# One 512-column product issued as two of 256: the input projections of a hybrid decoder layer on one Trainium2 core

## The chip, the cores and the metric

The kernel runs on one core of one Trainium2 chip. The metric is the device time of one execution in microseconds (us). The kernel before was run three times: 1012.82 us is the median, 1004.70 and 1013.37 us are the ends.

## What is computed

One decoder layer on 512 tokens of width 1024, in float32. It has three sublayers, each closed by a layer norm: a hybrid mixer, cross-attention into 256 memory tokens, and a SwiGLU channel mixer. Only the first one matters here. Cut to its input side:

```python
def hybrid_mixer(x, w_in, b_in, pool_w, ...):
    z = x @ w_in + b_in                       # 1024 -> 8 * 1024 columns
    z_pool, z_lru, z_b, z_c, z_h, z_gate = split(z)
    y_pool = multiscale_pool(z_pool, pool_w, pool_scale)   # grouped 256x256 products
    y_lru = rg_lru(z_lru, ..., w_r, b_r, w_i, b_i, ...) @ lru_w_out   # 128x128 gate heads
    y_conv = gated_short_conv(z_b, z_c, z_h, sconv_w, sconv_w_out)
    gates = sigmoid(z_gate).reshape(s, 3, 1024)
    merged = gates[:, 0] * y_pool + gates[:, 1] * y_lru + gates[:, 2] * y_conv
    return merged @ w_mix_out
```

## The kernel before

Every float32 product is made of three matmuls by the helper `mm3` (lines 843 to 847). Each operand is held as a high part and a low part (`wh`, `wl` for weights, `xT_h`, `xT_l` for the transposed tokens), and one product adds high x high (line 845), high x low (line 846) and low x high (line 847) into the same place of `ps`, the accumulators (8 banks of 512 float32 on 128 partitions). The first argument of each matmul is the stationary operand, a 128x128 block of weights, and the second is the moving operand, a number of token columns. In the trace each matmul has a weight load of its own in front of it, so one `mm3` is three weight loads and three matmuls.

The mixer's input side runs as four passes `a_pass(i)`, i = 0 to 3, each over two blocks of 128 columns of each of the branches (stage A, from 11.6 to 246.5 us of the profiled span). A pass consists of fifteen weight steps in a fixed order: lru0, lru1, pool0, pool1, P1, P5, P6, P2, P7, pool_w, ri, b0, P4, b1, P3. They come in two kinds:

- The steps whose names begin with lru, pool and b are done by `half_unit`: one call goes through 2 column blocks (`l`) and 4 blocks of the inner dimension (`k`), so it makes 8 `mm3`, each with all 512 tokens as moving columns. The steps pool_w (`p_h`, `p_l` moving) and ri (`vr_h`, `vr_l` moving) make 4 `mm3` each, also over 512 tokens, and stand in `a_pass` itself. In pass 0 the lru steps are done by another function, `half_tokens`, already 256 tokens at a time.
- The steps P1 to P7 are done by `product`: 8 `mm3` over 256 columns each (`x_part`, a quarter of `xT`, or sums of such quarters in `ta` and `tb`).

After stage A follow stage B (the gates, steps P1 to P7 again, all of 256 columns, to 374.6 us), the output projections (512 columns), the attention (both sizes), and the channel mixer, whose first part (665 to about 880 us, moving `x`, `xa`, `xb`, `xc`) is of 256 columns and whose second is of 512.

The order on each engine is written out by hand; each engine runs its own list and meets the others at semaphores. A weight step passes through a chain: a DMA brings it in (`raw`, `wx`), ScalarE writes the rounded high part (`wh`, lines 1354, 1410, 1466), VectorE subtracts to get the low part (`wl`, lines 1905, 1981, 2182). The weights have four slots. TensorE waits at the beginning of a step for its low part (`weights_ready`) and gives the slot free on the last matmul of the step (`weights_used`); ScalarE and VectorE also read the accumulators on that signal. So the last matmul of a step is the only one that anybody waits for.

Of the kernel before, what the change touches and what calls it, by code (L numbers as in the profile page):

```python
# [29 lines left out]
P = 128  # L30
# [29 lines left out]
def hybrid_layer(nc, x, mem, w_in, b_in, pool_w, pool_scale, lru_conv_w, lru_conv_b, lru_w_r, lru_b_r,  # L60
# [39 lines left out]
    with ExitStack() as ctx:  # L100
# [24 lines left out]
        xT_h = sb("xT_h", [P, KT, SEQ], F32R)  # L125
        xT_l = sb("xT_l", [P, KT, SEQ], F32R)
# [12 lines left out]
        with ExitStack() as scope:  # L139
            p_h = sb("p_h", [P, 2, SEQ], F32R, scope)  # L140
            p_l = sb("p_l", [P, 2, SEQ], F32R, scope)
            vr_h = sb("vr_h", [P, 2, SEQ], F32R, scope)
            vr_l = sb("vr_l", [P, 2, SEQ], F32R, scope)
# [82 lines left out]
        ps = ctx.enter_context(nc.psum_tensor("ps", [P, 8, 512], F32))  # L226
# [222 lines left out]
        def ri_bank(i, l, g):  # L449
            return A_POOL + g if l == 0 else m_bank(i) + 1 - g  # L450
# [391 lines left out]
        def _(pe):  # L842
            def mm3(dst, st, st_lo_part, mv_, mv_lo_part, start, stop, shared=False):

                nc.tensor.matmul(dst, st, mv_, start=start, stop=False, skip_group_check=shared)  # L845
                nc.tensor.matmul(dst, st, mv_lo_part, start=False, stop=False, skip_group_check=shared)  # L846
                return nc.tensor.matmul(dst, st_lo_part, mv_, start=False, stop=stop, skip_group_check=shared)  # L847
# [69 lines left out]
            def turn_par():  # L917
# [4 lines left out]
                nc.tensor.transpose(ps[:, 7, P:P + 32], rows[0:32, 1, :],  # L922
                                    ident[0:32, 0:32]).then_inc(par_full.sem, 1)

            def half_unit(i, name, bank):

                half = int(name[-1])
                weights_ready("A", 0, a_step(i, name))
                h_, l_ = (a_slot(w, i, name) for w in (wh, wl))
                for l in range(2):  # L930
                    for k in range(4):
                        last = mm3(ps[:, bank + l, :], h_[:, k, l * P:(l + 1) * P], l_[:, k, l * P:(l + 1) * P],
                                   xT_h[:, 4 * half + k, :], xT_l[:, 4 * half + k, :],
                                   half == 0 and k == 0, half == 1 and k == 3)
                last.then_inc(weights_used.sem, 1)

            def a_pass(i):
                j1 = i * 2 + 1
                low, mid = l_bank(i), m_bank(i)
# [38 lines left out]
                h_, l_ = (a_slot(w, i, "pool_w") for w in (wh, wl))  # L978
                for l in range(2):
                    for k in range(2):  # L980
                        last = mm3(ps[:, low + l, :], h_[:, k, l * P:(l + 1) * P], l_[:, k, l * P:(l + 1) * P],
                                   p_h[:, k, :], p_l[:, k, :], k == 0, k == 1)
                last.then_inc(weights_used.sem, 1)

                weights_ready("A", 0, a_step(i, "ri"))
# [2 lines left out]
                h_, l_ = (a_slot(w, i, "ri") for w in (wh, wl))  # L988
                for l in range(2):
                    for g in range(2):  # L990
                        if (l, g) == (1, 1):
                            pe.wait_ge(ac_sum.sem, ac_sum.done(3 * i))
                        last = mm3(ps[:, ri_bank(i, l, g), :], h_[:, g, l * P:(l + 1) * P], l_[:, g, l * P:(l + 1) * P],
                                   vr_h[:, l, :], vr_l[:, l, :], True, True)
                last.then_inc(weights_used.sem, 1)
                pe.wait_ge(ypool.sem, ypool.done(j1))
                half_unit(i, "b0", low)
# [145 lines left out]
            for k in range(4):  # L1143
                k_ready("C", 0, k, k)
                for t in range(TT):
# [6 lines left out]
                    last = accumulate("C", k, 2 * t, t, k == 0, False)  # L1152
# [21 lines left out]
            for h in range(HEADS):  # L1174
# [13 lines left out]
                for half in range(2):  # L1188
# [4 lines left out]
                    h_, l_ = (w_slot(w, "D", s).rearrange("p (k n) -> p k n", k=4) for w in (wh, wl))  # L1193
# [45 lines left out]
            for k, t in ((0, 2), (1, 2), (0, 3), (1, 3), (2, 2), (2, 3), (3, 2), (3, 3)):  # L1239
                if (k, t) == (0, 3):  # L1240
                    pe.wait_ge(ot_full.sem, ot_full.done(2 * HEADS - 1))
                last = accumulate("E", k, e_bank(t), t, k == 0, False)
# [1481 lines left out]
```

## Time and profile before

| | us |
|---|---|
| three runs: median (lowest, highest) | 1012.82 (1004.70, 1013.37) |
| span of the profiled execution | 1006.1 |
| TensorE (PE) busy | 991.6 (99% of the span) |
| weight loads (PEld) busy | 903.4 (90%) |
| VectorE (DVE) busy | 719.5 (72%) |
| ScalarE (ACT) busy | 503.5 (50%) |
| PE in the chain of work that ended last | 87% |

Busy time counts an engine as busy as long as at least one instruction is in it. Matmuls overlap: one of 512 columns is shown with 389 ns, yet the next one starts about 227 ns after it. So neither the busy share nor the duration of one matmul is its price in a row of matmuls; that is read from the starts of the first and the last of a row, and from their count. The granted clock of TensorE is shown in tenths or as a share of full speed. The profiled execution is one execution; its span lies between the lowest and the median run.

### The profile page before, as it was taken

Reading aid. Unit: us, or ns where it says so; the run is one execution under the profiler, and the core shown is the slowest. Engines: PE = TensorE matmul, PEld = TensorE weight load, DVE = VectorE, ACT = ScalarE, POOL = GpSimd, SP = SyncE. Lnnn points to the kernel's source line nnn. Section 1 sums busy time; section 2 is a strip of 40 time slices with the busy share of each in tenths; the row PEclk is TensorE's granted clock in tenths of the full one; section 3 lists DMA queues with packets and bytes.
Section 4 is the critical chain, followed back from the end, with each engine's and each line's share of the span. In section 5 each row is a group of like instructions: output and inputs, shape, how many; then the busy total and the mean of one; then the engine's idle time right before and its main releaser. Section 6 shows DMA issues by size and latency. Waiting matters only on the chain.

```text
span 1006.1 us, 15698 instructions
## 1 busy us (share of the span) xinstructions
PE 991.6 (99%) x6460; PEld 903.4 (90%) x6460; DVE 719.5 (72%) x909; ACT 503.5 (50%) x710; POOL 9.9 (1%) x22
## 2 busy tenths in 40 slices
PE   8999999999999999999999999999999999999997
PEld 8988889898999998888899998889999999988885
DVE  6979798796998885455675554589988888743336
ACT  6673846657575573123454443366554554623232
POOL 1000000000000000000000000000000000000000
PEclk9999999999999999999999999999999999999999
DMA  8243434315333344235163331223434332433212
GB/s 294 66 134 117 148 105 126 126 43 191 118 108 110 99 153 147 66 123 209 43 210 126 126 102 67 84 69 109 139 103 125 100 113 84 141 114 123 83 42 84
DMA packets 92165, 117.46 MB, mean 117 GB/s; under 512 B 3244, under 2 KB 82240, under 8 KB 92096
## 3 DMA queue, kind: packets, MB, share of 16 engines
q1 hardware_dynamic: 89328, 106.97, 32.6%
q0 software_dynamic: 2624, 9.47, 2.8%
q8 instruction: 50, 0.82, 0.3%
q14 instruction: 19, 0.16, 0.0%
q10 hardware_dynamic: 144, 0.05, 0.0%
HBM read 111.23 MB, written 5.24 MB: 116 GB/s over the span
## 4 chain that ended last, share of the span: by engine, by line
PE 87%; DVE 6%; ACT 4%; issue 2%; DMA 0%; DVEq 0%; POOL 0%; ACTq 0%; POOLq 0%
PE ps L845 28%; PE ps L846 28%; PE ps L847 28%; PE ps L874 1%; DVE wl L1981 1%; ACT wh L1410 1%; DVE o L2169 1%; ACT wh L1466 0%; DVE v L2031 0%; DVE wl L2182 0%; DMA raw<-in_w_in 0%; PE ps L1162 0%; PE ps L886 0%; ACT gates L1614 0%; ACT L1450 0%
## 5 line engine op out<-in xcount | busy, mean ns | idle before, releaser
L845 PE MATMUL ps<-xT_h,wh 128*128 128x256 f32 (+1 forms) x512 | 170.6, 333 | 0.4 <-DVE wl L1981 0.4
L846 PE MATMUL ps<-xT_l,wh 128*128 128x256 f32 (+1 forms) x512 | 169.8, 332 | 0.0
L847 PE MATMUL ps<-xT_h,wl 128*128 128x256 f32 (+1 forms) x512 | 169.7, 332 | 0.0
L1905 DVE TENSOR_TENSOR wl<-raw,wh 128x1024 fp32r<-128x1024 f32 x66 | 80.3, 1223 | 112.7 <-ACT wh L1354 112.7
L1354 ACT ACTIVATE wh<-raw 128x1024 fp32r<-128x1024 f32 x66 | 69.4, 1062 | 148.4 <-PE ps L847 136.2
L2182 DVE TENSOR_TENSOR wl<-raw,wh 128x1024 fp32r<-128x1024 f32 x72 | 87.5, 1223 | 54.3 <-ACT wh L1466 54.1
L1466 ACT ACTIVATE wh<-raw 128x1024 fp32r<-128x1024 f32 x72 | 75.5, 1058 | 96.7 <-PE ps L847 65.7
L845 PE MATMUL ps<-wh,st_h 128*128 128x512 f32 x304 | 118.8, 391 | 0.0
L847 PE MATMUL ps<-wh,st_l 128*128 128x512 f32 x304 | 118.3, 389 | 0.0
L846 PE MATMUL ps<-wl,st_h 128*128 128x512 f32 x304 | 118.3, 389 | 0.0
L845 PEld LDWEIGHTS ps<-xT_h,wh 128*128 128x128 f32 x512 | 96.2, 188 | 10.3 <-issue 0.8
L847 PEld LDWEIGHTS ps<-xT_h,wl 128*128 128x128 f32 x512 | 96.7, 189 | 9.5
L846 PEld LDWEIGHTS ps<-xT_l,wh 128*128 128x128 f32 x512 | 96.6, 189 | 9.3
L845 PE MATMUL ps<-xa,wh 128*128 128x256 f32 x368 | 101.9, 277 | 0.4 <-DVE xa L1921 0.4
L846 PE MATMUL ps<-xa,wh 128*128 128x256 f32 x368 | 101.6, 276 | 0.0
L847 PE MATMUL ps<-xa,wl 128*128 128x256 f32 x368 | 101.6, 276 | 0.0
L845 PEld LDWEIGHTS ps<-xa,wh 128*128 128x128 f32 x368 | 69.1, 188 | 1.0 <-DVE xa L1921 0.8
L847 PEld LDWEIGHTS ps<-xa,wl 128*128 128x128 f32 x368 | 69.1, 188 | 0.0
L846 PEld LDWEIGHTS ps<-xa,wh 128*128 128x128 f32 x368 | 69.1, 188 | 0.0
L847 PEld LDWEIGHTS ps<-wh,st_l 128*128 128x128 f32 x304 | 57.1, 188 | 11.8
L845 PEld LDWEIGHTS ps<-wh,st_h 128*128 128x128 f32 x304 | 57.1, 188 | 11.6
L846 PEld LDWEIGHTS ps<-wl,st_h 128*128 128x128 f32 x304 | 57.1, 188 | 11.6
(298 smaller groups left out, 2372.5 us busy)
## 6 DMA issues: line engine op xcount, KB each, us to landing
raw<-in_w_in SPq DMA_DIRECT2D x42, 512.0 KB, 3.8
raw<-in_ffn_w_down SPq DMA_DIRECT2D x11, 1024.0 KB, 4.9
raw<-in_ffn_w_gate SPq DMA_DIRECT2D x20, 512.0 KB, 4.1
wx<-in_w_in SPq DMA_DIRECT2D x16, 512.0 KB, 4.6
gb<-in_ffn_w_up SPq DMA_DIRECT2D x10, 512.0 KB, 3.9
raw<-in_ffn_w_up SPq DMA_DIRECT2D x10, 512.0 KB, 4.3
raw<-in_lru_w_out SPq DMA_DIRECT2D x8, 512.0 KB, 3.5
raw<-in_sconv_w_out SPq DMA_DIRECT2D x8, 512.0 KB, 3.4
```

Source lines behind the costliest of these rows:

```text
L845: nc.tensor.matmul(dst, st, mv_, start=start, stop=False, skip_group_check=shared)
L846: nc.tensor.matmul(dst, st, mv_lo_part, start=False, stop=False, skip_group_check=shared)
L847: return nc.tensor.matmul(dst, st_lo_part, mv_, start=False, stop=stop, skip_group_check=shared)
L874: last = nc.tensor.transpose(ps[:, bank + half, n * P:(n + 1) * P], src[:, tile, k * P:(k + 1) * P], ident[:])
L1354: nc.scalar.activation(w_slot(wh, phase, s, size), src, ACT.Copy).then_inc(w_hi.sem, 1)
L1410: nc.scalar.activation(a_slot(wh, i, name), a_src(i, name), ACT.Copy).then_inc(w_hi.sem, 1)
L1466: nc.scalar.activation(w_slot(wh, phase, n).rearrange("p (k n) -> p k n", k=4), src, ACT.Copy).then_inc(w_hi.sem, 1)
L1905: nc.vector.tensor_tensor(w_slot(wl, phase, s, size), src, w_slot(wh, phase, s, size).bitcast(F32), ALU.subtract).then_inc(w_lo.sem, 1)
L1981: nc.vector.tensor_tensor(a_slot(wl, i, name), a_src(i, name), a_slot(wh, i, name).bitcast(F32), ALU.subtract).then_inc(w_lo.sem, 1)
L2169: nc.vector.scalar_tensor_tensor(out=o[:, l, :], in0=ch[:, l, k:k + SEQ], scalar=par[:, SC_W0 + k, j:j + 1], in1=o[:, l, :], op0=ALU.mult, ...
L2182: nc.vector.tensor_tensor(w_slot(wl, phase, n).rearrange("p (k n) -> p k n", k=4), src, w_slot(wh, phase, n).rearrange("p (k n) -> p k n", ...
```

## The change

A new helper `by_tokens` takes the place of `mm3` in three places: in `half_unit`, in the step pool_w and in the step ri. It calls `mm3` twice, first for the columns of tokens 0 to 255, then for tokens 256 to 511, with the same block of weights. So three matmuls of 512 columns become six of 256, and three weight loads become six. `start` (which clears the place before the first addition) is given to the first half alone, as `product` does already; `stop` goes to both. Waits and signals stay where they were: the signal still stands on the last matmul of the step. No instruction of another engine is changed, and no DMA.

```diff
+            def by_tokens(bank, st, st_lo_part, mv_, mv_lo_part, start, stop):
+
+                for tok in range(2):
+                    part = slice(tok * 256, (tok + 1) * 256)
+                    last = mm3(ps[:, bank, part], st, st_lo_part, mv_[:, part], mv_lo_part[:, part],
+                               start and tok == 0, stop, shared=True)
+                return last
+
             def half_unit(i, name, bank):
...
                     for k in range(4):
-                        last = mm3(ps[:, bank + l, :], h_[:, k, l * P:(l + 1) * P], l_[:, k, l * P:(l + 1) * P],
-                                   xT_h[:, 4 * half + k, :], xT_l[:, 4 * half + k, :],
-                                   half == 0 and k == 0, half == 1 and k == 3)
+                        last = by_tokens(bank + l, h_[:, k, l * P:(l + 1) * P], l_[:, k, l * P:(l + 1) * P],
+                                         xT_h[:, 4 * half + k, :], xT_l[:, 4 * half + k, :],
+                                         half == 0 and k == 0, half == 1 and k == 3)
...
                     for k in range(2):
-                        last = mm3(ps[:, low + l, :], h_[:, k, l * P:(l + 1) * P], l_[:, k, l * P:(l + 1) * P],
-                                   p_h[:, k, :], p_l[:, k, :], k == 0, k == 1)
+                        last = by_tokens(low + l, h_[:, k, l * P:(l + 1) * P], l_[:, k, l * P:(l + 1) * P],
+                                         p_h[:, k, :], p_l[:, k, :], k == 0, k == 1)
...
-                        last = mm3(ps[:, ri_bank(i, l, g), :], h_[:, g, l * P:(l + 1) * P], l_[:, g, l * P:(l + 1) * P],
-                                   vr_h[:, l, :], vr_l[:, l, :], True, True)
+                        last = by_tokens(ri_bank(i, l, g), h_[:, g, l * P:(l + 1) * P], l_[:, g, l * P:(l + 1) * P],
+                                         vr_h[:, l, :], vr_l[:, l, :], True, True)
```

In the list of TensorE the first place that is changed is the beginning of step pool0 in pass 0. Before, the last two matmuls of step lru1 (256 columns, by `half_tokens`) are followed by the first product of pool0, whose first matmul waits for the low part of the weights:

```order
L846 MATMUL ps<-xT_l,wh 128x256
L847 MATMUL ps<-xT_h,wl 128x256
L845 MATMUL ps<-xT_h,wh 128x512 [waits w_lo]
L846 MATMUL ps<-xT_l,wh 128x512
L847 MATMUL ps<-xT_h,wl 128x512
```

Now the same place reads:

```order
L846 MATMUL ps<-xT_l,wh 128x256
L847 MATMUL ps<-xT_h,wl 128x256
L845 MATMUL ps<-xT_h,wh 128x256 [waits w_lo]
L846 MATMUL ps<-xT_l,wh 128x256
L847 MATMUL ps<-xT_h,wl 128x256
L845 MATMUL ps<-xT_h,wh 128x256
L846 MATMUL ps<-xT_l,wh 128x256
L847 MATMUL ps<-xT_h,wl 128x256
```

Three rows have become six, and from here to the end of stage B TensorE's list holds no matmul of 512 columns up to the first output projection. The second place is step pool_w of the same pass, behind the last product of P7 (`tb` moving). Before:

```order
L845 MATMUL ps<-tb,wh 128x256
L846 MATMUL ps<-tb,wh 128x256
L847 MATMUL ps<-tb,wl 128x256
L845 MATMUL ps<-p_h,wh 128x512 [waits zl_full,p_lo,w_lo]
L846 MATMUL ps<-p_l,wh 128x512
L847 MATMUL ps<-p_h,wl 128x512
```

And now:

```order
L845 MATMUL ps<-tb,wh 128x256
L846 MATMUL ps<-tb,wh 128x256
L847 MATMUL ps<-tb,wl 128x256
L845 MATMUL ps<-p_h,wh 128x256 [waits zl_full,p_lo,w_lo]
L846 MATMUL ps<-p_l,wh 128x256
L847 MATMUL ps<-p_h,wl 128x256
L845 MATMUL ps<-p_h,wh 128x256
L846 MATMUL ps<-p_l,wh 128x256
L847 MATMUL ps<-p_h,wl 128x256
```

The wait is the same and stands on the same matmul; behind it, each product has twice the rows.

## Rows read from the trace of the kernel before

**Rows 1.** The page: busy time of TensorE, then the chain's shares by engine.
```profile
PE 991.6 (99%) x6460; PEld 903.4 (90%) x6460; DVE 719.5 (72%) x909; ACT 503.5 (50%) x710; POOL 9.9 (1%) x22
...
PE 87%; DVE 6%; ACT 4%; issue 2%; DMA 0%; DVEq 0%; POOL 0%; ACTq 0%; POOLq 0%
```

**Rows 2.** Groups by line and shape, PE: count | busy us, mean ns | idle before.
```profile
L845 PE MATMUL ps<-xT_h,wh 128*128 128x512 f32 x240 | 93.9, 391 | 0.2 <-DVE wl L1981 0.2
...
L845 PE MATMUL ps<-xT_h,wh 128*128 128x256 f32 x272 | 76.7, 282 | 0.2 <-DVE wl L1981 0.2
...
L845 PE MATMUL ps<-p_h,wh 128*128 128x512 f32 x16 | 6.4, 399 | 0.1
...
L845 PE MATMUL ps<-vr_h,wh 128*128 128x512 f32 x16 | 6.2, 389 | 0.0
```

**Rows 3.** Timeline of PE: first and last of 96 matmuls of 512 columns, pass 3.
```profile
191.35 0.40 PE L845 MATMUL ps<-xT_h,wh 128*128 128x512 f32 x1
...
212.91 0.39 PE L847 MATMUL ps<-xT_h,wl 128*128 128x512 f32 x1
```

**Rows 4.** Timeline of PE: first and last of 120 matmuls of 256 columns, pass 2.
```profile
155.19 0.28 PE L845 MATMUL ps<-xT_h,wh 128*128 128x256 f32 x1
...
169.20 0.28 PE L847 MATMUL ps<-tb,wl 128*128 128x256 f32 x1
```

**Rows 5.** Timeline of PE: first and last of 48 of 256 columns (P2, P7), pass 1.
```profile
105.93 0.28 PE L845 MATMUL ps<-xT_h,wh 128*128 128x256 f32 x1
...
111.26 0.28 PE L847 MATMUL ps<-tb,wl 128*128 128x256 f32 x1
```

**Rows 6.** Timeline of PE: first and last of the next 24 of 256 columns (P4).
```profile
122.28 0.28 PE L845 MATMUL ps<-tb,wh 128*128 128x256 f32 x1
...
124.99 0.28 PE L847 MATMUL ps<-tb,wl 128*128 128x256 f32 x1
```

**Rows 7.** Timeline of all engines: matmuls (PE) and weight loads (PEld) inside P2, pass 2.
```profile
165.08 0.28 PE L845 MATMUL ps<-xT_h,wh 128*128 128x256 f32 x1
165.08 0.19 PEld L846 LDWEIGHTS ps<-xT_l,wh 128*128 128x128 f32 x1
...
165.20 0.28 PE L846 MATMUL ps<-xT_l,wh 128*128 128x256 f32 x1
```

**Rows 8.** Timeline of PE: its waits from 25 to 375 us [idle before <- releaser].
```profile
61.83 0.36 PE L845 MATMUL ps<-tb,wh 128*128 128x256 f32 x1 [1.00 <-DVE wl L1981]
...
73.40 0.47 PE L845 MATMUL ps<-xT_h,wh 128*128 128x512 f32 x1 [0.21 <-DVE wl L1981]
...
103.09 0.38 PE L845 MATMUL ps<-ta,wh 128*128 128x256 f32 x1 [1.99 <-ACT o L1532]
...
261.21 0.36 PE L845 MATMUL ps<-tb,wh 128*128 128x256 f32 x1 [0.44 <-DVE wl L2182]
```

**Rows 9.** The chain in order of time, 225 to 262 us: two of its pieces.
```profile
230.80 0.68 ACT act L1525
...
259.85 1.23 DVE wl L2182
```

**Rows 10.** Busy time by stretch: columns PE, PEld, DVE, ACT, POOL, PEclk, DMA, GB/s.
```profile
191.35:213.14 21.79, 21.79 (x99) 18.02 (x97) 19.91 (x23) 8.80 (x11) 0.00 (x0) 1.00 0.37 121
...
246.48:363.47 116.99, 116.48 (x986) 116.01 (x984) 103.52 (x110) 70.97 (x103) 0.00 (x0) 1.00 0.34 105
700.00:800.00 100.00, 100.00 (x885) 100.00 (x884) 86.85 (x87) 53.78 (x66) 0.00 (x0) 1.00 0.38 117
```

**Rows 11.** Groups by line and shape: the channel mixer's matmuls of 256 columns, line 845.
```profile
L845 PE MATMUL ps<-xa,wh 128*128 128x256 f32 x368 | 101.9, 277 | 0.4 <-DVE xa L1921 0.4
...
L845 PE MATMUL ps<-xb,wh 128*128 128x256 f32 x160 | 44.2, 276 | 0.0
...
L845 PE MATMUL ps<-xc,wh 128*128 128x256 f32 x80 | 22.1, 276 | 0.0
...
L845 PE MATMUL ps<-x,wh 128*128 128x256 f32 x16 | 4.4, 276 | 0.0
```

## The prediction, made before the changed kernel ran

> **What bounds the kernel now.** I read the page first: TensorE is busy for 99% of the span and holds 87% of the chain of work that ended last [rows 1]. So the price of the change is first the price of its matmuls. The page cannot give that price, because matmuls overlap: the groups by line and shape show 389 to 399 ns for one of 512 columns and 282 ns for one of 256 [rows 2], and with these two splitting would cost 2 x 282 - 391 = 173 ns. I therefore went to the timeline and divided the time between the first and the last start of a row of like matmuls by their number less one. What the reader is to see there:
>
> - 512 columns: 96 in a row, (212.91 - 191.35) / 95 = 227.0 ns from start to start [rows 3].
> - 256 columns, the usual step in stages A and B: 120 in a row, (169.20 - 155.19) / 119 = 117.7 ns [rows 4]. Call it the slow step.
> - 256 columns, a second value: (111.26 - 105.93) / 47 = 113.4 ns [rows 5]. Call it the fast step. 100 us of the channel mixer show it as well, 100 / 885 = 113.0 ns [rows 10].
>
> Both steps occur with the same operands (`xT`, `tb`), and the granted clock is 1.00 (2.4 GHz) in 117 us of slow steps as in 100 us of fast ones [rows 10], so it is not the clock. The fast one in stage A starts right behind the wait of 1.99 us at 103.09 [rows 8], survives the change of operand from P2 to P7 [rows 5], and is gone after the next matmuls of 512 columns: P4 of the same pass runs at (124.99 - 122.28) / 23 = 117.8 ns [rows 6]. So TensorE seems to fall into one of two steps and to stay in it until something disturbs it. Twice the fast step is 226.8 ns, the price of one matmul of 512 columns; twice the slow one is 8.4 ns more. That is the whole question of this change.
>
> **What the change adds.** The products touched are 22 calls of `half_unit` with 8 each (four in pass 0, six in each later pass), 16 of pool_w and 16 of ri: 208 products, 624 matmuls of 512 columns. The groups agree: 240 x 512 on `xT` of which 176 are these, and 16 each on `p_h` and `vr_h`, per line of three [rows 2]. So 624 matmuls and 624 weight loads are added: 120 in pass 0 and 168 in each of passes 1 to 3. Their waits, signals and neighbours stay; DMA queues and other engines get nothing new.
>
> *Weight loads.* A load has 0.19 us, more than the 0.118 us between two starts, but it begins together with the matmul in front of it (both at 165.08) and the next matmul follows at 165.20 [rows 7]. The loads are hidden behind the matmul before, at 256 columns too, and their cost is in the step already. The Trainium skill (TensorE: Matmul & The Clock Gate, The mechanism) says that a load overlaps matmuls in flight only where it goes to other row groups; all loads here fill all rows, so by that rule each added load would stand alone, and with the page's P / 1.2 (107 ns for 128 columns) the sum would be an estimated +67 us. Rows 7 speak against the rule here.
>
> *Price of one split.* Slow step: 2 x 117.7 - 227.0 = +8.4 ns. Fast step: 2 x 113.4 - 227.0 = -0.2 ns. These are the two bounds. The same skill page (Back-to-back issue gap) gives N / 2.4 + 2.5 ns, which is 215.8 and 109.2 ns, so +2.6 ns a split and an estimated +1.6 us in all; both its levels lie below the rows (227.0 and 117.7), so the rows are used.
>
> I take the slow step: stage B stands in it from end to end (116.99 us / 986 = 118.7 ns, small gaps within [rows 10]), and so do the matmuls behind the wait of 0.44 us for weights at 261.21 [rows 8], which lies inside that stretch. All 624 then cost 624 x 8.4 = 5.2 us of TensorE time.
>
> **What of it lies on the path.** Waits of TensorE swallow what comes before them, as long as what they wait for is not itself made late by TensorE [rows 8].
>
> - To 61.83: 96 splits (pool0, pool1, pool_w, ri, b0), 0.8 us, against a wait of 1.00 us for low weights. VectorE, which makes these, is busy with its own list; a part may leak through pool_w's result. I put 0.1 us.
> - To 73.40: 24 splits, 0.2 us against 0.21 us. Zero.
> - To 103.09: 96 splits, 0.8 us against 1.99 us. Zero.
> - From there to 230.80: no wait, TensorE is the chain. Pass 1 has 72 left, pass 2 168, pass 3 108 up to the end of pool_w: 348 x 8.4 = 2.9 us, all on the path.
> - At 230.80 the chain leaves TensorE for ScalarE (it reads pool_w) and comes back by the low weights of 259.85 [rows 9]; TensorE meets them at 261.21 with 0.44 us to spare [rows 8]. The last 60 splits are 0.5 us: 0.1 us on the path.
> - Stage B and later: nothing changed, everything 3 us later, weights and sums too.
>
> Sum: 0.1 + 2.9 + 0.1 = **+3.1 us**, 1006.1 -> 1009.2 for the profiled execution.
>
> **Against the runs.** The profiled span is 6.7 us below the median run and close to the lowest one. The two steps offer a reason: the channel mixer has 3 x (368 + 160 + 80 + 16) = 1872 matmuls of 256 columns [rows 11], here in the fast step; in the slow one they would take 1872 x 4.3 ns = 8.0 us more, and the runs lie 8.1 to 8.7 us apart (1004.7 against 1012.82 and 1013.37). This is an inference. On it, the median is an execution with a slow channel mixer, and the change does not touch that: 1012.8 + 3.1 = **1015.9 us**. With a fast one it would be about 1008.
>
> **The rivals.**
>
> 1. *The fast step takes hold in stage A.* For: the change takes away the 512-column rows behind which the slow step was found again [rows 6], and one row of the fast step lasted over two products [rows 5]. Against: most entries gave the slow one, and pool_w and ri bring other operands each pass, for which no row shows a 256-column step. Splits then cost nothing, and the matmuls that were of 256 columns already gain: between 111 and 230 us there are 48 + 168 + 120 = 336, x 4.3 ns = -1.4 us, and what is won before 261.21 beyond that meets the low weights there. I put -1.7 us: 1011.1 us.
> 2. *It carries on through stage B.* As 1, but the entry at 261.21 is fast too (there it was slow, behind a wait [rows 8]). Some 900 more matmuls x 4.3 ns = -3.9 us: together -5.6, 1007.2 us on the median, 999 with a fast channel mixer.
> 3. *The loads are not covered* where the token half changes, so that the step there is a whole load, 188 ns, not 117.7. For it: a load of 0.19 us is longer than a step. Against: rows 4 and 7, and `product` changes halves in the middle without a gap. 624 x (2 x 188 - 227) = +93 us, near 1106 us. It decides from a step of about 125 ns on (408 splits behind 103 us x 23 ns = 9.4 us). The skill's rule on row groups, above, belongs to this rival.
> 4. *Nothing to be seen:* the waits swallow it all. It would need 3 us of waits after 103.09; there are 0.44 [rows 8]. 1012.8 us.
>
> **How the numbers follow.** Forecast 0.55, rival 1 0.25, rival 2 0.10, rival 3 0.04, rival 4 0.06. About 1% (10 us) is what a measurement of this kernel can tell from no change. Forecast and rivals 1 and 4 lie within it; each can also come with a median whose channel mixer is fast, 8 us lower, which I give one chance in three. Below 1002.7 us then lie rival 2 and a part of rival 1 in that case: 0.06 faster. Above 1023 us lie rival 3 and a forecast at a price above its bound: 0.06 slower. Same: 0.88. The range goes from rival 1 with a fast channel mixer (1011.1 - 8 = 1003) to the forecast with all 624 splits on the path and another 2 us (1012.8 + 5.2 + 2 = 1020).
>
> **What the profile of the changed kernel would show.** TensorE with 624 more matmuls and loads. The start-to-start step in pool0, b0 and b1: 117.7 ns confirms the price, 113.4 ns means rival 1. The waits at 61.83, 73.40 and 103.09 shorter by 0.8, 0.2 and 0.8 us, that at 261.21 gone. The start of stage B, 246.48 now, some 3.4 us later. The step in the channel mixer tells which of the two kinds of execution was profiled. I am wrong if a gap stands at each change of halves, if pool_w or ri show a third step, or if the channel mixer's step is set by what happens in stage A.

## The result, and the profile after

Twenty runs of the changed kernel, against twenty of the kernel before (the three of the table above among them), have a median of 1010.08 us (1009.49 to 1013.27) against 1006.17 us (1004.70 to 1016.28). The ratio is 1.004 with a 95% interval of 1.0027 to 1.0053: the change makes the kernel slower by 0.4%, +3.9 us, which is more than this many runs are uncertain by and less than the 1% that the prediction had set as the bound of "no change". The sum had been +3.1 us. The median of 1012.82 us that the prediction started from was that of three runs; of twenty it is 6.7 us lower.

The profiled execution of after has a span of 1008.0 us (1006.1 before). Its page, to be held against [rows 1]:

```profile
span 1008.0 us, 16946 instructions
...
PE 996.3 (99%) x7084; PEld 932.8 (93%) x7084; DVE 719.5 (71%) x909; ACT 502.6 (50%) x710; POOL 9.9 (1%) x22
```

TensorE has 624 more matmuls and loads (7084 against 6460), as announced, and nothing else has grown. Line numbers behind the new helper are 8 higher than before. Where the time went is read from the timeline of PE in after, at the same matmuls as in [rows 3 to 8] (columns: start, duration, engine, line, operation, tiles, shape; in brackets the idle time ahead and who ended it):

```profile
50.27 0.39 PE L845 MATMUL ps<-p_h,wh 128*128 128x256 f32 x1
...
62.49 0.36 PE L845 MATMUL ps<-tb,wh 128*128 128x256 f32 x1 [0.46 <-DVE wl L1989]
...
74.06 0.35 PE L845 MATMUL ps<-xT_h,wh 128*128 128x256 f32 x1
...
103.74 0.38 PE L845 MATMUL ps<-ta,wh 128*128 128x256 f32 x1 [0.78 <-ACT o L1540]
...
123.50 0.28 PE L845 MATMUL ps<-tb,wh 128*128 128x256 f32 x1
...
194.99 0.28 PE L845 MATMUL ps<-xT_h,wh 128*128 128x256 f32 x1
...
217.91 0.28 PE L847 MATMUL ps<-xT_h,wl 128*128 128x256 f32 x1
...
235.03 0.28 PE L845 MATMUL ps<-vr_h,wh 128*128 128x256 f32 x1
...
266.37 0.28 PE L845 MATMUL ps<-tb,wh 128*128 128x256 f32 x1
...
289.21 0.28 PE L845 MATMUL ps<-xT_h,wh 128*128 128x256 f32 x1
...
302.70 0.28 PE L847 MATMUL ps<-ta,wl 128*128 128x256 f32 x1
...
365.37 0.39 PE L845 MATMUL ps<-lru_h,wh 128*128 128x512 f32 x1
```

Of before one more line is needed, the first matmul of ri of pass 3:

```profile
230.01 0.39 PE L845 MATMUL ps<-vr_h,wh 128*128 128x512 f32 x1
```

What is to be seen there, as lateness against the same matmul of before:

- 61.83 has become 62.49 (+0.66) and 103.09 has become 103.74 (+0.65). The waits of [rows 8] have shrunk from 1.00 to 0.46, from 0.21 to nothing, and from 1.99 to 0.78 us, and all the same the start behind the first is 0.66 us later.
- From there the lateness grows evenly: 122.28 to 123.50 (+1.22), 191.35 to 194.99 (+3.64), and 230.01 to 235.03 (+5.02, the first matmul of ri of pass 3).
- The price is in 194.99 and 217.91: these are the first and last of 192 split matmuls, the ones of [rows 3]. (217.91 - 194.99) / 191 = **120.0 ns** from start to start. That is neither the slow step (117.7) nor the fast one (113.4), but a third. pool_w and ri show it too (119.2 to 120.0, apart from pool_w of pass 0, which has a gap in it), while all P steps of the stage stay at 117.8 or 113.3. Two such matmuls cost 2 x 120.0 - 227.0 = +13.0 ns, where I had +8.4.
- 261.21 has become 266.37 (+5.16); the wait of 0.44 us there is gone.
- Then 3.3 us are given back. From about 286 us on stage B runs at the fast step: 120 matmuls from 289.21 to 302.70, 13.49 / 119 = 113.4 ns, which in the execution of before were slow. The output projections begin at 365.37, 1.9 us later than before (363.47), and that is the difference to the end: 1008.0 - 1006.1 = 1.9.

The busy time by stretch says the same of stage B (columns as in [rows 10]):

```profile
246.48:363.47 116.99, 116.93 (x1018) 116.72 (x1017) 104.09 (x110) 73.44 (x107) 0.00 (x0) 1.00 0.35 112
...
297.37:360.00 62.63, 62.63 (x555) 62.63 (x554) 55.40 (x57) 41.91 (x66) 0.00 (x0) 1.00 0.36 110
```

62.63 us / 555 = 112.8 ns with the granted clock at 1.00 (2.4 GHz), where the whole stretch of before gave 118.7 ns at the same clock. So the profiled executions differ by 1.9 us, but with the same step in stage B they would differ by 1.9 + 3.3 = 5.2 us. The difference of the two medians, 3.9 us, lies between these.

Why the first wait did not swallow its part is in the timelines of ACT and DVE. In pass 0 ScalarE reads the accumulators of P1 (`o`) and right behind them those of pool0 and pool1 (`u`), and VectorE's next work on them is a scan over `u`. Before, then the low weights that end the wait at 61.83:

```profile
38.21 0.84 ACT L1532 ACTIVATE o<-ps,par 128x256 f32<-128x256 f32 x2 [0.41 <-PE ps L847]
...
38.94 1.27 ACT L1514 ACTIVATE u<-ps,par 128x512 f32<-128x512 f32 x2
39.73 1.22 DVE L2048 TENSOR_TENSOR_SCAN ws<-u 128x512 f32<-128x512 f32 x1
...
60.46 1.22 DVE L1981 TENSOR_TENSOR wl<-wx,wh 128x1024 fp32r<-128x1024 f32 x1
```

The same in after:

```profile
38.89 0.84 ACT L1540 ACTIVATE o<-ps,par 128x256 f32<-128x256 f32 x2 [0.85 <-PE ps L847]
39.62 1.27 ACT L1522 ACTIVATE u<-ps,par 128x512 f32<-128x512 f32 x2
40.39 1.23 DVE L2056 TENSOR_TENSOR_SCAN ws<-u 128x512 f32<-128x512 f32 x1 [0.33 <-issue]
...
61.13 1.21 DVE L1989 TENSOR_TENSOR wl<-wx,wh 128x1024 fp32r<-128x1024 f32 x1
```

TensorE's P1 stands behind the 48 splits of pool0 and pool1 (48 x 13.0 = 0.62 us), so ScalarE waits longer for it and begins its two reads 0.68 us late. VectorE had no wait at the scan before; now it waits 0.33 us there and begins it 0.66 us late. From there its list runs on 0.66 to 0.67 us late, to the low weights that TensorE waits for at 62.49. The wait there is for a chain that TensorE itself had made late.

### The profile page after: what moved, and what is told of

Its sections match the earlier page's. It is cut to its first block, busy times and chain, and to the rows that moved or that the text cites. A ratio compares the mean times of both kernels' runs of the same rounds, so it can differ in the third digit from the quotient of the medians.

```text
span 1008.0 us, 16946 instructions
## 1 busy us (share of the span) xinstructions
PE 996.3 (99%) x7084; PEld 932.8 (93%) x7084; DVE 719.5 (71%) x909; ACT 502.6 (50%) x710; POOL 9.9 (1%) x22
## 4 chain that ended last, share of the span: by engine, by line
PE 87%; DVE 6%; ACT 5%; issue 2%; DVEq 0%; POOL 0%; ACTq 0%; POOLq 0%
PE ps L845 28%; PE ps L846 28%; PE ps L847 28%; PE ps L874 1%; DVE wl L1989 1%; ACT wh L1474 1%; ACT wh L1418 1%; DVE wl L2190 1%; DVE o L2177 1%; DVE v L2039 0%; PE ps L1170 0%; PE ps L886 0%; ACT gates L1622 0%; ACT L1458 0%; ACT L1448 0%
## 5 line engine op out<-in xcount | busy, mean ns | idle before, releaser
L845 PE MATMUL ps<-xT_h,wh 128*128 128x256 f32 (+1 forms) x688 | 201.0, 292 | 1.2 <-DVE wl L1989 1.2
L847 PE MATMUL ps<-xT_h,wl 128*128 128x256 f32 (+1 forms) x688 | 200.2, 291 | 0.0
L846 PE MATMUL ps<-xT_l,wh 128*128 128x256 f32 (+1 forms) x688 | 200.2, 291 | 0.0
L1913 DVE TENSOR_TENSOR wl<-raw,wh 128x1024 fp32r<-128x1024 f32 x66 | 80.3, 1223 | 112.8 <-ACT wh L1362 112.8
L845 PEld LDWEIGHTS ps<-xT_h,wh 128*128 128x128 f32 x688 | 131.1, 191 | 4.0 <-issue 1.6
L847 PEld LDWEIGHTS ps<-xT_h,wl 128*128 128x128 f32 x688 | 130.6, 190 | 2.6
L846 PEld LDWEIGHTS ps<-xT_l,wh 128*128 128x128 f32 x688 | 130.6, 190 | 2.4
L847 PE MATMUL ps<-wh,st_l 128*128 128x512 f32 x304 | 118.3, 389 | 0.0
L846 PE MATMUL ps<-wl,st_h 128*128 128x512 f32 x304 | 118.3, 389 | 0.0
```

Source lines behind the costliest of these rows:

```text
L1913: nc.vector.tensor_tensor(w_slot(wl, phase, s, size), src, w_slot(wh, phase, s, size).bitcast(F32), ALU.subtract).then_inc(w_lo.sem, 1)
```

## The experiments

In the expectations "stage B begins at" names the start of step P3 of pass 3, the last step of stage A (246.48 us before, 252.24 after); it is this same point that all kernels are compared at. The first four runs look for what makes 120.0 ns out of 117.8 among the things that `half_unit` does and `product` does not.

### 1. The token half as the outermost loop

```diff
-                for l in range(2):
-                    for k in range(4):
-                        last = by_tokens(bank + l, ...)
+                for l, k, tok in [(l, k, tok) for tok in range(2) for l in range(2) for k in range(4)]:
+                    last = one_half(bank + l, tok, ...)
```

The same in pool_w and ri. Each block of weights is now used a second time only after all the others.

> The same 624 additional matmuls of 256 columns, but the token half is the outermost loop of a step (half, column block, inner block): no half is changed from product to product, and no block of weights is loaded twice in a row. In the changed kernel the step inside these products is 120.0 ns (5.64 us for 47 matmuls). If it comes from the changing halves or from the weights that are loaded twice in a row, it is 117.8 or 113.3 ns here, stage B begins at about 250 us instead of 252.2, and the time lies 1.8 us (117.8) to 4 us (113.3) under that of the changed kernel. If any split of these products costs 120.0 ns, stage B begins at 252.2 us and nothing is gained.

First and last of 144 matmuls of lru1, pool0 and pool1 of pass 3, timeline of PE of this kernel:

```profile
201.17 0.28 PE L845 MATMUL ps<-xT_h,wh 128*128 128x256 f32 x1
...
218.33 0.28 PE L847 MATMUL ps<-xT_h,wl 128*128 128x256 f32 x1
```

(218.33 - 201.17) / 143 = 120.0 ns. P3 of pass 3 begins at 252.65 us. The order of the halves, which here is that of `product`, is not the cause. (Times: 1010.13, 1010.60, 1021.01 and 1021.27 us, ratio 1.0085, interval 1.0024 to 1.0146; what lies behind the two values comes with run 4.)

### 2. No block of weights twice in a row

```diff
+for l, k, tok in [(l, kk + dk, tok) for l in range(2) for kk in (0, 2) for dk, tok in ((0, 0), (1, 1), (0, 1), (1, 0))]:
```

> The halves change with every product as in the changed kernel, but neighbouring products use different blocks of weights (inner block 0 with half 0, block 1 with half 1, block 0 with half 1, block 1 with half 0). If the step of 120.0 ns comes from the same weights being loaded twice in a row, it falls to 117.8 ns or less; if it comes from the changing halves (of what is read or of what is written), it stays at 120.0.

Measured: lru0 of pass 3 has its 48 matmuls from 194.72 to 200.36 us, 5.64 / 47 = 120.0 ns; P3 at 251.96; one run, 1009.53 us. That the weights are loaded again right away is not the cause.

### 3. Both halves read the same tokens

```diff
-                    last = mm3(ps[:, bank, part], st, st_lo_part, mv_[:, part], mv_lo_part[:, part],
+                    last = mm3(ps[:, bank, part], st, st_lo_part, mv_[:, 0:256], mv_lo_part[:, 0:256],
```

> As the changed kernel, but both halves read the columns of tokens 0 to 255 as moving operand (so the second half of the tokens is not computed); the written half still changes and the weights are still loaded twice in a row. If the changing half of what is read makes the 120.0 ns, the step is 117.8 ns or less here; if it is the written half or the weights, it stays at 120.0.

Measured: lru0 of pass 3 from 195.24 to 200.88 us, again 120.0 ns; one run, 1010.03 us.

### 4. Both halves written to the same place

```diff
-                    last = mm3(ps[:, bank, part], st, st_lo_part, mv_[:, part], mv_lo_part[:, part],
+                    last = mm3(ps[:, bank, 0:256], st, st_lo_part, mv_[:, part], mv_lo_part[:, part],
```

> As the changed kernel, but both halves are added into columns 0 to 255 of the accumulators (so the sums are not the reference's); the read half still changes and the weights are still loaded twice in a row. If the changing written half makes the 120.0 ns, the step is 117.8 ns or less here; if it is the read half or the weights, it stays at 120.0.

Measured: 120.0 ns again. So neither the tokens read nor the columns written matter, and none of the four things tried about the halves makes the third step. But this execution took 1021.17 us (span 1019.4), and its timeline shows the other thing that I had inferred from rows: stage B stayed in the slow step (+5.2 us late at its end, where after is +1.9), and so did the channel mixer. First and last of 240 of its matmuls:

```profile
700.61 0.28 PE L845 MATMUL ps<-xa,wh 128*128 128x256 f32 x1
...
728.76 0.28 PE L847 MATMUL ps<-xb,wl 128*128 128x256 f32 x1
```

28.15 / 239 = 117.8 ns, with the same program there as in after and before, where it ran at 113 ns. The two slow stretches account for the time: after's 1009.8 (profiled execution) + 3.3 for stage B + 8.2 for the channel mixer = 1021.3. So one program's executions differ by these amounts without any change to it, and the 8.0 us of the prediction's inference is real.

### 5. The place of the weights in their slot

Reading the kernel again for a difference between `half_unit` and `product` left one that is not in the loops. `w_at` (lines 373 to 380) lets the weights of the lru, pool and b steps begin at word 48 of their slot (192 bytes), those of all other steps of stage A at word 0. The slots begin at multiples of 256 bytes, and so do `p_h` and `vr_h`; `xT`, `ta`, `tb`, `xa`, `xb` and `xc` lie 192 bytes behind such a multiple. So in `half_unit`, pool_w and ri weights and moving operand begin at the **same place modulo 256 bytes**, and in the P steps 192 bytes apart. The rows from which I had taken the price of a 256-column matmul [rows 4, 5, 10] are all of the second kind. (The four slots lie 4352 bytes apart, 17 x 256 and no multiple of 512, and the step is the same in all four; that is why I count modulo 256.)

```diff
-                return 48 if A_ORDER[n % A_BODY][:-1] in ("lru", "pool", "b") else 0
+                return 0
```

This is after, with the weights of the split units at word 0; pool_w and ri are left as they were.

> The changed kernel, but the weights of the steps lru, pool and b lie at word 0 of their slot, as those of P1 to P7 do, not at word 48. (With 48 words, 192 bytes, the blocks of weights and the moving columns of xT begin at the same place modulo 256 bytes; with 0 they begin 192 bytes apart, as in the steps P.) If the relative place of the two operands sets the step, these steps now run at 117.8 or 113.3 ns and pool_w and ri stay at 120.0; stage B begins 1.5 us (117.8) or more earlier than in the changed kernel (252.2 us). If the kind of step (its place in the program, what it writes) sets it, 120.0 stays everywhere.

The same 192 matmuls of pass 3 as above, then P3 and the wait for low weights, timeline of PE of this kernel:

```profile
190.72 0.28 PE L845 MATMUL ps<-xT_h,wh 128*128 128x256 f32 x1
...
212.36 0.28 PE L847 MATMUL ps<-xT_h,wl 128*128 128x256 f32 x1
...
245.44 0.28 PE L845 MATMUL ps<-xT_h,wh 128*128 128x256 f32 x1
...
260.12 0.36 PE L845 MATMUL ps<-tb,wh 128*128 128x256 f32 x1 [0.92 <-DVE wl L2190]
```

21.64 / 191 = 113.3 ns: the third step is gone, and here it is the fast one that took its place (in pass 1 up to the wait near 103 us the same units run at the slow one, 117.8); pool_w and ri, whose weights lie at word 0 and their moving operand too, kept 119 to 120.0. P3 begins at 245.44, 6.8 us before after and 1.0 before before. Median 1006.63 us (1003.83 to 1015.13) against 1008.30 for the kernel before in the same comparison, ratio 0.9974 (0.9931 to 1.0017): against before the times show no difference.

### 6. pool_w and ri moved apart as well

```diff
-                return 48 if A_ORDER[n % A_BODY][:-1] in ("lru", "pool", "b") else 0
+                return 16 if A_ORDER[n % A_BODY] in ("pool_w", "ri") else 0
```

> As the run before, and the weights of pool_w and ri lie at word 16, so that in every step of stage A the weights and the moving columns begin 192 bytes apart modulo 256. If the place alone sets the step, no step of 120.0 ns is left in stage A, also not in pool_w and ri; the step that stage A is in is then no longer changed by these steps, and the fast one (113.3 ns), which begins behind the wait at 103 us, may last to stage B: it would begin at about 245 us instead of 252.2, and the time would be 3 to 5 us under that of the changed kernel. If it falls back to 117.8 ns, stage B begins at about 250 us.

From 103 us on pool_w and ri run at 117.6 to 117.8 ns, everything else of stage A at 113.3 (the step right behind ri at 113.7).

```profile
245.80 0.28 PE L845 MATMUL ps<-xT_h,wh 128*128 128x256 f32 x1
...
260.55 0.35 PE L845 MATMUL ps<-tb,wh 128*128 128x256 f32 x1 [0.99 <-DVE wl L2190]
```

Against before the wait behind it has grown from 0.44 to 0.99 us, so the matmul at 261.21 starts only 0.66 us earlier. Median 1006.04 us (1003.78 to 1012.17), ratio 0.9965 (0.9932 to 0.9999).

### 7. Nothing split, but the P steps put to the bad place

This is the kernel before, with the weights of P1 to P7 of stage A at word 48, the place of the moving operand.

```diff
-                return 48 if A_ORDER[n % A_BODY][:-1] in ("lru", "pool", "b") else 0
+                return 0 if A_ORDER[n % A_BODY] in ("pool_w", "ri") else 48
```

> The kernel before (512 columns, nothing split), but the weights of P1 to P7 in stage A lie at word 48 as well, so the same place modulo 256 bytes as the moving columns. If the place sets the step, the matmuls of 256 columns of P1 to P7 run at 120.0 ns instead of 117.8 (28 steps, 672 matmuls, 1.5 us or more of TensorE time), without any split. If the split itself makes it, they stay at 117.8 or 113.3.

First and last of the 48 matmuls of P5 and P6 of pass 3:

```profile
217.03 0.28 PE L845 MATMUL ps<-ta,wh 128*128 128x256 f32 x1
...
222.68 0.28 PE L847 MATMUL ps<-ta,wl 128*128 128x256 f32 x1
```

5.65 / 47 = 120.2 ns, 117.8 before; the 512-column matmuls of lru, pool and b stay at 226.7 to 227.9 where no wait stands in them. P3 begins at 247.83 (+1.35). So the 120 ns come with the place and without any split. (One run: 1006.01 us.)

### 8. A scan of the place

After, with the weights of the steps of stage A at words 0 to 60 in steps of 4.

```diff
+                c = 13 * (n // A_BODY) + [m for m in A_ORDER if m not in ("pool_w", "ri")].index(name)
+                return 4 * (c * (5, 7, 11, 13)[c // 16] % 16)
```

> The changed kernel, with another place of the weights in their slot for each step of stage A: 0 to 60 words in steps of 4, each place about three times, behind different places. If the place sets the step, the start-to-start times group by place: 120.0 at 48 words, 117.8 or 113.3 at 0, and others between. If history sets it, the same place shows different steps behind different places.

Mean steps by place, rows with a wait left out: word 0 113.4 to 117.8 ns; words 4 and 8 118.6 to 118.9; 12 to 24 118.3 to 120.0; 28 to 40 116.6 to 118.2; 44 117.3 to 120.0; 48 119.8 to 120.0; 52 to 60 117.8 to 118.5. So words 12 to 24 and 44 are as slow at times as the same place, and 36 and 40 lie below 117.8. In this scan only word 0, 192 bytes apart, reached the fast step. (One run: 1012.47 us.) Two steps that follow each other on the same operands, the first at word 44, the second at word 0:

```profile
85.47 0.28 PE L849 MATMUL ps<-xT_h,wh 128*128 128x256 f32 x1
...
91.11 0.28 PE L851 MATMUL ps<-xT_h,wl 128*128 128x256 f32 x1
91.22 0.28 PE L849 MATMUL ps<-xT_h,wh 128*128 128x256 f32 x1
...
96.55 0.28 PE L851 MATMUL ps<-xT_h,wl 128*128 128x256 f32 x1
```

5.64 / 47 = 120.0 ns and 5.33 / 47 = 113.4 ns. The place alone does not tell which of 113.3 and 117.8 word 0 has; what came before it must count too.

### 9. What sets the step of a row at word 0

Run 6, with every second step over a part of stage B and of the channel mixer at one of the words 4 to 60.

```diff
+            if B0 + 8 <= n < B0 + 43 and (n - B0) % 2:
+                return 4 * ((n - B0) // 2 * 7 % 15) + 4
+            if F0 + 8 <= n < F0 + 70 and (n - F0) % 2:
+                return 4 * ((n - F0) // 2 * 7 % 15) + 4
```

> The kernel of the run e6 (stage A with all operands 192 bytes apart modulo 256), and in stage B and in the channel mixer every second step of weights lies at another place of its slot (4 to 60 words), the steps between at word 0. Question: does the place before decide whether the next step at word 0 runs at 113.3 or at 117.8 ns? If it does, each place is followed by the same step each time that it occurs (113.3 behind 44 words, 117.8 behind 48 and 36, as seen in the scan). If the two steps at word 0 are a matter of chance at each entry, the same place is followed by both.

Within this run a step at word 0 has the same speed each time behind the same place, in stage B and in the channel mixer: 113.3 to 114.3 ns behind words 4, 8, 12, 20, 24, 36, 40, 44 and 60, and 117.8 behind 16, 28, 48 and 52; behind 56 it stays as it was. (Behind 32, seen from the fast step alone, it was fast.) One expectation failed: behind word 36 I had 117.8 from the scan, and here all three steps behind it were fast. Word 32, 64 bytes apart, has both steps itself: 113.3 ns in its three steps here, 117.7 to 117.8 in the scan. Four steps in a row, at words 0, 24, 0 and the next one, starts of the first matmul of each:

```profile
788.19 0.28 PE L849 MATMUL ps<-xa,wh 128*128 128x256 f32 x1
...
791.02 0.29 PE L849 MATMUL ps<-xa,wh 128*128 128x256 f32 x1
...
793.89 0.28 PE L849 MATMUL ps<-xb,wh 128*128 128x256 f32 x1
...
796.61 0.28 PE L849 MATMUL ps<-xb,wh 128*128 128x256 f32 x1
```

With 24 matmuls each: 117.9 ns at word 0, 119.6 at word 24, and then 113.3 at word 0. One step at a chosen place turns the slow step into the fast one. It is not a full rule: behind matmuls of 512 columns the step after word 24 was slow all the same, and word 36 was followed by 117.8 in the scan and by 113.3 here. (One run: 1011.88 us.)

### 10. Nothing split, all weights at word 0

```diff
-                return 48 if A_ORDER[n % A_BODY][:-1] in ("lru", "pool", "b") else 0
+                return 0
```

This is the kernel before: here the lru, pool and b steps with their 512 columns leave word 48.

> The kernel before, nothing split, but the weights of lru, pool and b at word 0 instead of 48, so that the matmuls of 512 columns too read weights and moving columns that begin 192 bytes apart. If the place works on 512 columns as on 256, their step is more than 226.7 ns here (up to 2 x 117.8 = 235.6), and the place at word 48 of the kernel before is the right one for 512 columns and the wrong one for 256. If 512 columns do not mind, it stays at 226.7 to 227.9 ns.

First and last of 72 matmuls of lru1, pool0 and pool1 of pass 3:

```profile
197.24 0.39 PE L845 MATMUL ps<-xT_h,wh 128*128 128x512 f32 x1
...
213.80 0.40 PE L847 MATMUL ps<-xT_h,wl 128*128 128x512 f32 x1
```

16.56 / 71 = 233.2 ns against 226.7 to 227.0 at word 48. For 512 columns the same place is the good one, for 256 the bad one: word 48 fitted the uncut products and was left in place when they were cut. The P steps ran fast in this execution (113.3 to 113.9; P7 of pass 1 alone at 117.8), so P3 begins at 247.02, only 0.5 us late. (One run: 1005.30 us.)

### 11. The split with chosen places

Run 6, with three steps (two in stage B, one at the beginning of the channel mixer) at word 44 to bring the fast step about.

```diff
+            if n in (B0 + 5, B0 + 13, F0 + 4):
+                return 44
```

> The kernel of the run e6 (the split of the changed kernel, all operands of stage A 192 bytes apart modulo 256), and three steps of weights at word 44: two in stage B (the sixth and the fourteenth step) and the fifth of the channel mixer. The run e9 showed 113.3 ns behind each step at word 44. If the place of the step before sets the step and not chance, stage B behind the fourteenth step and the channel mixer behind the fifth run at 113.3 ns in every execution: the output projections begin at about 359 us (363.5 before), the span is about 1002 us, and the time is about 1003.5 us with runs within 1 us, against 1005 to 1016 us of the kernel before. If it is chance, a part of the runs stays 3 or 8 us above the others.

Median 1004.99 us of 12 runs, all between 1003.90 and 1006.49, against 1008.17 of 23 runs of before (1004.53 to 1017.36): ratio 0.9954 (0.9925 to 0.9984). The output projections of the profiled execution (span 1002.3):

```profile
359.52 0.39 PE L847 MATMUL ps<-lru_h,wh 128*128 128x512 f32 x1
```

They begin 3.95 us before the 363.47 of before. Stage B is at 117.8 ns ahead of the first of its steps at word 44 (263.16) and at 113.3 from behind it; the channel mixer was at 113.3 in this execution already before its own step at word 44. The place and the span came as expected; the median is 1.5 us above the 1003.5 expected, and the runs spread over 2.6 us and not 1, but none lies 3 or 8 us above the others. By the interval this version is 0.2 to 0.8% faster than the kernel before. The changed kernel did not run beside it; the shortest of its twenty runs, 1009.49 us, is longer than the longest of these twelve.

### 12. The same without the split

The kernel before, with P1 of stage A at word 44 (to bring the fast step about behind the 512 columns) and the same three steps.

```diff
+                if A_ORDER[n % A_BODY] == "P1":
+                    return 44
...
+            if n in (B0 + 5, B0 + 13, F0 + 4):
+                return 44
```

> The kernel before, nothing split (512 columns at word 48), with the same three steps at word 44 in stage B and the channel mixer, and P1 of each pass at word 44 too. If the split itself is worth something once the places are right, this kernel is slower than the run before it by up to 1 us; if the gain comes from the places alone, the two agree within 1 us. P5, P6, P2 and P7 of each pass should run at 113.3 ns here, P4 and P3 at 117.8.

Median 1005.21 us of 12 runs (1004.24 to 1006.13), ratio 0.9967 (0.9941 to 0.9992). The channel mixer of its profiled execution shows the three steps turned over at work. The first and last of 48 matmuls ahead of the step at word 44, and of 24 behind it:

```profile
681.63 0.28 PE L849 MATMUL ps<-x,wh 128*128 128x256 f32 x1
...
687.17 0.28 PE L851 MATMUL ps<-xa,wl 128*128 128x256 f32 x1
...
690.15 0.28 PE L849 MATMUL ps<-xa,wh 128*128 128x256 f32 x1
...
692.76 0.28 PE L851 MATMUL ps<-xa,wl 128*128 128x256 f32 x1
```

5.54 / 47 = 117.9 ns and 2.61 / 23 = 113.5 ns; the rest of the channel mixer stays at 113.3, some 190 us long. Runs 11 and 12 differ by 0.2 us with overlapping runs: once the places are chosen for each, the split itself does nothing that can be seen. What they gain on before is the places, and with them the long executions: nine of the 23 of before lie from 1012.88 to 1017.36 us, and none of the 24 of runs 11 and 12 is over 1006.49.

The profile of run 12 also shows where some of the remaining spread comes from. Behind its wait of 2.09 us near 103 us TensorE ran for 1.4 us at a granted clock of 1.00, and then the clock fell to 0.50 (1.2 GHz) for 3.4 us:

```profile
104.20:107.60 3.40, 3.40 (x18) 3.40 (x17) 3.33 (x5) 0.62 (x2) 0.00 (x0) 0.50 0.00 0
```

There the starts lie 213 ns apart, which costs this execution 1.5 us (15 x 100 ns); it is the longest of its twelve. The eight of them with a granted share of 0.997 over the whole execution took 1005.10 to 1006.13 us, the four with 0.998 or 0.999 took 1004.24 to 1004.61. That those eight all hold such a stretch is inferred, since one alone was profiled.

## Why the prediction was right or wrong, point by point

**The price of one split: wrong, and this is the step that failed.** I priced it at +8.4 ns and called the slow and the fast step the two bounds. The row shows +13.0 (2 x 120.0 - 227.0), above both. The bounds were from rows of the P steps, which move the same `xT` over weights at another place of their slot. Their duration, shape, clock and operand names were like those of the new matmuls, the addresses were not, and `w_at` stood in the code. Run 5 takes the step away by the address alone, run 7 makes it without a split, and runs 1 to 4 exclude the order of the halves, the repeated weights, the tokens read and the columns written. The prediction's own sign of being wrong, "if pool_w or ri show a third step", came true, and `half_unit` showed it too.

**The path from 103.09 to 230.80: right in kind.** There is no wait, and every split is on the path: 348 of them made (5.02 - 0.65) = 4.4 us, 12.6 ns each. (My 2.9 us had the same count with 8.4 ns.)

**The waits: two right, one wrong.** At 103.09 the wait gave 1.2 us, which is 96 x 13 ns, and swallowed all of it; at 73.40 it was used up. At 61.83 I put 0.1 us for what may leak through pool_w's result, and it was 0.66 us by another way: pool0 and pool1 stand ahead of P1, and the whole of their 0.62 us went into the chain that the wait is for, at ScalarE's reads behind P1 and VectorE's scan at 40.39, before pool_w had begun. That a chain may be made late by TensorE itself was named, but the place was wrong and the size was not worked out, though the 48 splits could be counted. At 261.21 the wait is gone, as forecast, and gave 0.6 us back.

**The sum.** 0.66 + 4.4 + 0.1 = 5.2 us at 266.37, where I had 3.1. Then stage B ran in the fast step in after's profiled execution and in the slow one in that of before, so that 1.9 us are left at the end. This is no effect of the split that I can show: after too is slow from 266 to 283 us and changes only behind a gap of 0.2 us. Before changes at the same place too (113.5 ns from 279.12 to 281.05) and falls back behind its next gap, at 281.39. The twenty runs of after lie in two groups, fourteen from 1009.49 to 1010.44 and six from 1012.51 to 1013.27. They are 3 us apart, the price of stage B's step (3.3). That the groups are these two kinds of execution is inferred from the sizes. The measured +3.9 us is near my +3.1 by luck: a sum too low by 2.1 us (1.5 of it the price, 0.6 the first wait) met a mix of executions that was on average about 1.3 us kinder to after. The clock of run 12 may have a part in that: all twenty runs of after have a granted share of 0.998 or 0.999, while 23 of the 49 runs of before beside the experiments have 0.996 or 0.997. No trace of before shows such a stretch, so this stays open.

**The base: wrong, the other step that failed.** That the channel mixer's step takes 8 us more in some executions was right; run 4 has one with the rows. That the median is such an execution was wrong: of twenty runs of before, twelve lie from 1004.70 to 1006.5. Three runs of a time with several values do not give its median. The predicted 1015.9 is 5.8 us above what was measured for this reason, with the error of price going the other way.

**The bound of "no change": wrong.** I held that a measurement of this kernel cannot tell less than about 1% (10 us) from no change, and gave "same" 0.88. Twenty runs of each told 0.4% from it: the interval of the ratio, 1.0027 to 1.0053, is 2.6 us wide and leaves out 1.

**The rivals.** Rival 1 (the fast step takes hold in stage A) did not occur, since at the place where the split units lie no fast step was seen, in the scan or elsewhere. With the place changed it did: runs 5 and 6 are what it described, P3 at 245.4 and 245.8 instead of 246.48, and the gain largely met the wait for low weights, as the prediction said of it. Rival 2 occurred in stage B alone, in some executions, not as a consequence of stage A. Rival 3 (loads not covered) is refuted: no split matmul stands behind a load of 188 ns; the step is 120.0, and run 2, which never uses a block twice in a row, has the same. The Trainium skill (TensorE: Matmul & The Clock Gate, The mechanism) says in one place that a load overlaps matmuls in flight only where it goes to other row groups, and by that a load of all rows would stand alone; these rows disagree with it, as [rows 7] did. The same section also lets a load into a background weight buffer be pulled ahead of matmuls in flight, which the prediction left out; with that the rows agree, but no run here shows the buffer. Rival 4 would have needed waits behind 103.74 that are not there.

**What stays open.** What collides inside the chip when weights and moving operand begin at the same place is not shown by any run; that the place decides it is. Nor is it shown what chooses the step at the entries of stage B and of the channel mixer in an execution. Behind the point near 260 us where stage B waits for low weights, or waited before the split, every profiled kernel but run 12 was slow. At the channel mixer's entry near 665 us it was slow in runs 4, 5, 6 and 12 and fast in the others, with the same instructions in all of them up to the fifth step of the channel mixer.

## What to carry to other kernels

A price read from a row holds for the new instructions only if their operands lie alike: compare the start addresses of weights and moving operand (here modulo 256 bytes), not only shape, engine and tile. When the shape of a matmul is changed, its operands' places are to be chosen again, for what suits 512 columns (the same place, 226.7 against 233.2 ns) was among the worst for 256 (120.0 against 113.3 or 117.8). A wait swallows lateness only where the chain that it waits for does not start behind the late work; count what stands ahead of that start.

## What the hardware showed that was not expected

At a granted clock of 1.00 and with the same shape (128x256, three matmuls to a product, a load of 128x128 ahead of each) TensorE has three steps at the places that the two kernels use: 113.3, 117.8 and 120.0 ns. The third comes where weights and moving operand begin at the same place modulo 256 bytes, split or not (runs 5 and 7). Of the other two, which are both seen 192 bytes apart, TensorE keeps one for up to about 200 us (117.8 ns from 683 to 890 us in run 4), through changes of operands and weights. What turned it over in these traces was matmuls of 512 columns, a wait, or one step of weights at another place, such as 176 bytes into the slot in runs 8, 9, 11 and 12. In this kernel the choice is worth 3.3 us in stage B and 8.2 us in the channel mixer, together more than the change that was to be measured.
